# Another order of the first mixer's steps on four engines

## The chip, the cores and the metric

The kernel runs on one core of a Trainium2 chip. A core has a matrix engine (TensorE, PE in the rows, with PEld its weight loads), a vector engine (VectorE, DVE), an engine for functions of one element (ScalarE, ACT), a general one (GpSimd, POOL), and a fifth, SyncE (SP), that here only issues transfers. The metric is the time of one execution on the device in microseconds, the median of three runs.

## The reference, cut to what matters

The program is one block with a three-part mixer and a feed-forward network, and then two layers with three branches each. Only the order of work in the first mixer changes. There 272 tokens of 1024 features are normalised, multiplied by `w_in` and split into three groups:

```python
p = rms_norm(h, norm_mix_pre[l]) @ w_in[l]
pa = p[..., :A_COLS]                  # 512 columns: the LRU group
pb = p[..., A_COLS:A_COLS + B_COLS]   # 1544 columns: forgetting attention, 8 heads
pc = p[..., A_COLS + B_COLS:]         # 1024 columns: RWKV-7, 4 heads
oa = rg_lru_group(xa, ya, ...)        # a convolution, two gates, a scan, gelu
ob = forgetting_attention_group(...)  # softmax(q k + c_i - c_j) v
oc, v_own = rwkv7_group(pc, ...)      # a recurrent state per head
mixed = jnp.concatenate([oa, ob, oc], axis=-1) @ w_out[l]
h = h + rms_norm(mixed, norm_mix_post[l])
```

The recurrence of RWKV-7 is

```python
s_kk = jnp.einsum('bhij,bhj->bhi', S, kk_t)
S = S * w_t[:, :, None, :] - s_kk[..., None] * (kk_t * a_t)[:, :, None, :] + v_t[..., None] * k_t[:, :, None, :]
```

The kernel computes it in chunks of 64 tokens. Five chunks of four heads need the inverse of a triangular 64x64 matrix each, found in five levels of doubling (blocks of 2, 4, and so on up to 64).

## The kernel before, in words

All weights of the matrix products come from memory as units of 128x1024 numbers. SP fetches a unit into `raw`, ACT rounds it to `whi`, DVE (or POOL, for every fourth unit in the mixer) subtracts to get the rest `wlo`, and PE multiplies three times, `xh` by `whi`, `xl` by `whi` and `xh` by `wlo`. These are the steps called `split`, letter w. One output tile of 128 features takes one unit and 24 matmuls. The three products serve to keep float32 accuracy.

The mixer's tiles come in the order C (8 tiles, RWKV), two heads' q and k, v, the other q and k, and A (4 tiles, LRU); then the 8 tiles of `w_out`, called `op`. Between the tiles PE does the small products of the three groups.

No scheduler runs. Each engine executes a list of steps, and the table `WEAVE` holds the order: for each phase and engine one string of letters. `mixer_lines` gives for each letter a line of steps, and `laid` takes the next step of the line that each letter names. So a string fixes how the lines are interleaved on an engine, never the order inside a line. The letters are: d tiles and their evacuations from PSUM, w splits, r the RWKV steps in their order of need, s RWKV steps with time to spare, l and n the LRU, f the forget gates, e and o the attention turns (even and odd, six turns of five parts: scores, maximum and exponentials, reciprocal and normalisation, transposes, values), m token shifts, c the late copies before `w_out`, p the `w_out` tiles, z `beat`.

Semaphores carry the dependences: `wait_ge` in a step waits for named events, `says` announces one. A wait blocks everything that stands behind it on its engine. PSUM has 8 banks. Tiles rotate through three of them, all small products through the other five, and a product waits until its bank's earlier holder was read.

The steps that matter here:

- `enter` ("in", k): for each k of 8, ACT scales `h` to `xh` and squares it, DVE makes `xl`, PE does nine matmuls and sums the squares. `inend` is the square root on ACT and the reciprocal `rr` on DVE, which every evacuation needs.
- `la.a`, `la.c`: constants of the LRU, on ACT (absolute value, exponential, logarithm) and DVE.
- `rw.X`: the first matrix of the inverse, from `rw_be` and `AR`. `rw.inv0`: its transpose `rw_XT`, on POOL. `rw.lb`: the masks of the levels (`rw_x` tiles, from `MA`), the first on DVE, the rest on POOL.
- `rw.leva`, level v: 40 matmuls (20 per half) and two copies on ACT. `rw.levb`: 80 matmuls and four subtractions on DVE from `rw_X` and `rw_XT`, the "level differences".
- `lr.conv`, `lr.exp`, `lr.tan`, `lr.b`, `lr.scan`, `lr.cut`: the LRU group, on DVE, ACT and POOL.
- `rw.pair`, `rw.scanU`, `rw.scanS`, `rw.o`, `rw.mean`, `rw.var`, `rw.fin`, `rw.oc`: the rest of RWKV. `late`: the attention's output copied and split for `w_out`.
- `beat`: 1 to 4 products of a matrix of ones with itself, whose result nobody reads, 12 in the seven that letter z places (BEATS 3, 1, 1, 2, 1, 1, 4), and 4 more inside the first `op` tile. Each is executed as two matmuls in the trace. `pulse` is the same kind of work, 14 products ahead of the feed-forward part.

Of the kernel before, what the change touches and what calls it, by code (L numbers as in the profile page):

```python
# [261 lines left out]
WEAVE = {  # L262
    "mixer": {
        "pe": (
            "ddddddddddfdddddddddrddddddrrdddddddrrrddddfdddddddrrddeddrrrsssdrdrdlrdrdldrddrssrseeessseosoorre"
            "eerrrrrrozrororeroozrerereeozozrorrroeozerrzorzrroppppppppp"
        ),
        "act": (
            "eodwdwdddwwddwdsdndwwwwfwwrwsrwwrwrrrrwrrwwwrrwwdddddwwrrwwserewlrwlwlrdwdresslseesocorrrererooooo"
            "eeceoooeeroerroerrrrroocccpwwpwppwpwpwpwpp"  # L270
        ),
        "dve": (
            "dmwdwdddwwwdddsdnddwddfwwwdmdfdwwmwsrrddmdmmdwwrdwmmwwmddwdrrwrrrrdwwdrsssdfwrrrwerwrrrwddssrdreee"
            "edlrwdlrrwldwwldrrssssslssoolllrroererrrerrororooreroooerrcerereooreoeroorrrrcccpwwpwwpppwpwpwpp"
        ),
        "pool": (
            "wwewwedmoopdddddddwdwwwmmwwwwmmwwwwrrmrmmwwwwrrrwwwwsswrrrwwreeeweerrwwwwllcoooooeeeeeoooooceeeooo"
            "rrcpppwwwwpppp"
        ),
        "sp": (  # L280
            "dwwwwwwwwwwwwwwwwwwwwwwwwwwwwwwwwwwww"
# [7 lines left out]
        "act": (
            "wddddqddwddwbwdwccwccwvwccwvvwccwvvwcwvvccwwvcvwcwvcwvcwcwvvwcwvvcwcwvcvwcwvcwvcwcwvvwcwvvcwccvwvw"  # L290
            "cwvcvwcwcvwvcwcwvvwqccwvvwcvwqvqccwcvwvwcvwcvcwwvcvwvwvwvbwwwwwwwwwww00w00w01w00111111000001111w1w"
            "wrrr"
        ),
        "dve": (
            "hwdhhhhdhddhhddwddwwdddwddwcdwcdwvcwdcdwvcwdcwdvcdwcwdvcwdcwdvwcdwcdwvcdwcwdvcwdcwdvcwdcwdvwcdwcdw"
            "vcwdcwdvcwdcdvwcwdcwvdcwdcwdvwcdwcdwvcwdcdwvcdwcvwdcdwcdvwcwdcvwdcdwcwdvcwcvwccvwwwwwwwwwwwww0000w"
            "0011w0101110w1101000011111www"
        ),
# [13 lines left out]
        "act": (
            "aeoswwwwwwtwtwwtwwweedwdddodowdwedddowwdwdeeowdowdeedwweoodweedeeowdwboodeoeeodwweedwdwwwwwwwoooew"
            "essssosssowwowwoddddwsdwdwsdwdwdwdwdwdwdwdwdwdwdwdwdwdwdwdwdwdwwwmwmwwmwmwwmwmwwmwmbwwww000w00w1w0"
            "11011110001111100wrrwwr"
        ),
        "dve": (
            "ddwwdwdwdwdwdwttddwwdwdwdeeowdeeowdodddddwwowdwydwyeodwydeoyewdeeyodwwyoeedeywedoyewodwooydeoyeedw"
            "weedyyuwwuwuwuwwwowoosseowssssosswowwoddddsdwwdsdwwdwdwdwdwdwdwdwdwdwdwdwdwdwdwdwdwdwddwddwddwmddw"
            "mddwddwmddwmddwddwmddwmddwddwmwmwwww0000w0011w11011001110000w111110www"  # L320
        ),
# [13 lines left out]
        "act": (
            "aoewswwwwtwwtwwtwwweeddddoodwdewdddowwwdwdeeooweewddeooweewdeoedwdwoodbeoeeowdeeowwwoodeoeodwowdww"
            "wowwwswssssswswwdsddddwwsdwdwdwdwdwdwdwdwdwdwdwdwdwdwdwdwdwdwdwwwmmwwwmwmwwmwmwwmmbwwww0000011111"
        ),
# [2405 lines left out]
```

How the kernel before makes its waits and increments, by code:

```python
    def wait_ge(self, *events):  # L118
        if self.book.counting:
            return
        for ev in events:
            name, val = self.book.value[ev]
            if self.met.get(name, 0) < val:
                self.e.wait_ge(self.book.sem(name), val)
                self.met[name] = val
# [612 lines left out]
            def bank(banks, key):  # L738
                b, before = book.take(banks, key)
                if before is not None and not book.counting:
                    pe.wait_ge(*book.freed_by[before])
                return tiles[b]
# [1 line left out]
            def take(n=1):  # L744
                u, i = divmod(at[0], 8)
                at[0] += n
                if u == 0 and i == 4 or u and i == 0:
                    pe.wait_ge(("w.hi", u), ("w.lo", u))
                c = slice(128 * i, 128 * (i + n))
                return whi[:, u % NSPL, c], wlo[:, u % NSPL, c], [("w.used", u)] if at[0] % 8 == 0 else []
# [1 line left out]
            def dense(o, xs, event, first=True, last=True):  # L752
                for i, (a, b, evs) in enumerate(xs):
                    hi, lo, said = take()
                    pe.wait_ge(*evs)
                    mm(o, hi, a, first and i == 0, False)
                    mm(o, hi, b, False, False)
                    t = mm(o, lo, a, False, last and i == len(xs) - 1)
                    if last and i == len(xs) - 1:
                        said = [event] + said
                    if said:
                        t.then_inc(*pe.says(*said))
```

## Time and profile before

| what | value |
|---|---|
| median of three runs | 941.23 us (940.35 to 943.87) |
| the profiled execution, from its first to its last instruction | 940.6 us |
| PE busy | 918.4 us, 98% of the span |
| DVE busy | 696.6 us, 74% |
| ACT busy | 521.6 us, 55% |
| POOL busy | 226.8 us, 24% |
| the mixer, to the end of the last `w_out` tile | 0 to 196 us |

The page gives the profiled execution no time other than this span. A row of a timeline gives start, duration, engine, line and operation, and in brackets the idle time before it with what ended it. Since the ends of matmuls are modelled, idle time of PE is better read from brackets and from starts than from the busy sum. Most DVE and POOL rows carry the line of a helper (L1713, L1717, L1718, L1721, L2306), so the tiles' names tell the steps apart.

### The profile page before, as it was taken

Reading aid. Unit: us, or ns where it says so; the run is one execution under the profiler, and the core shown is the slowest. Engines: PE = TensorE matmul, PEld = TensorE weight load, DVE = VectorE, ACT = ScalarE, POOL = GpSimd, SP = SyncE. Lnnn points to the kernel's source line nnn. Section 1 sums busy time; section 2 is a strip of 40 time slices with the busy share of each in tenths; the row PEclk is TensorE's granted clock in tenths of the full one; section 3 lists DMA queues with packets and bytes.
Section 4 is the critical chain, followed back from the end, with each engine's and each line's share of the span. In section 5 each row is a group of like instructions: output and inputs, shape, how many; then the busy total and the mean of one; then the engine's idle time right before and its main releaser. Section 6 shows DMA issues by size and latency. Waiting matters only on the chain.

```text
span 940.6 us, 19615 instructions
## 1 busy us (share of the span) xinstructions
PE 918.4 (98%) x7924; PEld 855.0 (91%) x7924; DVE 696.6 (74%) x1072; ACT 521.6 (55%) x942; POOL 226.8 (24%) x194
## 2 busy tenths in 40 slices
PE   8999999989999999999999999999899999999997
PEld 7999887979999988789999899998699998999995
DVE  6988875477999896578788695586768787665684
ACT  8653464446655664464665475545646665555442
POOL 2445321441212221004222040032023122410240
PEclk9999999999999999999999999999999999999999
DMA  8543200235555555456544446555284435555451
GB/s 320 180 157 113 70 26 2 68 113 180 183 189 185 184 178 180 170 176 245 179 140 153 152 136 203 192 188 181 100 305 152 146 125 177 183 178 181 159 201 45
DMA packets 41705, 150.32 MB, mean 160 GB/s; under 512 B 4624, under 2 KB 5008, under 8 KB 41360
## 3 DMA queue, kind: packets, MB, share of 16 engines
q1 hardware_dynamic: 39600, 141.54, 44.7%
q10 hardware_dynamic: 2016, 7.54, 2.1%
q8 instruction: 63, 1.03, 0.4%
q14 instruction: 26, 0.21, 0.1%
HBM read 148.01 MB, written 1.05 MB: 158 GB/s over the span
## 4 chain that ended last, share of the span: by engine, by line
PE 89%; DVE 4%; ACT 2%; issue 2%; DMA 1%; POOL 1%; DVEq 0%; SPq 0%; ACTq 0%; POOLq 0%
PE ps L736 87%; PE ps L1073 2%; DVE wlo L1713 1%; DMA raw<-in_ws 1%; DVE S L1713 1%; ACT whi L1297 1%; PE ps L1189 0%; DMA h<-in_hT 0%; ACT xh L1297 0%; DVE xl L1721 0%; POOL ocf L2306 0%; ACT L1297 0%; ACT tmp L1297 0%; DVE ht L1721 0%; DVE pcraw L1713 0%
## 5 line engine op out<-in xcount | busy, mean ns | idle before, releaser
L1297 ACT ACTIVATE whi<-raw 128x1024 fp32r<-128x1024 f32 (+1 forms) x265 | 278.2, 1052 | 282.1 <-PE ps L736 276.5
L736 PE MATMUL ps<-xh,whi 128*128 128x256 f32 (+2 forms) x1440 | 412.9, 287 | 4.5 <-ACT xh L1297 1.8
L736 PE MATMUL ps<-xl,whi 128*128 128x256 f32 (+2 forms) x1440 | 407.9, 283 | 2.3 <-DVE xl L1721 2.2
L736 PE MATMUL ps<-xh,wlo 128*128 128x256 f32 (+2 forms) x1440 | 407.0, 283 | 0.0
L1713 DVE TENSOR_TENSOR wlo<-raw,whi 128x1024 fp32r<-128x1024 f32 (+1 forms) x257 | 328.0, 1281 | 103.8 <-ACT whi L1297 103.1
L736 PEld LDWEIGHTS ps<-xh,whi 128*128 128x128 f32 x1440 | 271.5, 189 | 10.9 <-issue 8.3
L736 PEld LDWEIGHTS ps<-xl,whi 128*128 128x128 f32 x1440 | 270.9, 188 | 3.9 <-DVE xl L1721 3.5
L736 PEld LDWEIGHTS ps<-xh,wlo 128*128 128x128 f32 x1440 | 272.0, 189 | 0.0
L736 PE MATMUL ps<-yh,whi 128*128 128x256 f32 x232 | 65.3, 282 | 0.0
L736 PE MATMUL ps<-yl,whi 128*128 128x256 f32 x232 | 65.2, 281 | 0.0
L736 PE MATMUL ps<-yh,wlo 128*128 128x256 f32 x232 | 65.2, 281 | 0.0
L2306 POOL TENSOR_TENSOR gts<-gts 128x256 f32<-128x256 f32 x32 | 33.2, 1047 | 132.0 <-DVE gts L1721 131.4
L2306 POOL TENSOR_TENSOR al<-cv,ah 128x256 fp32r<-128x256 f32 x22 | 30.2, 1374 | 117.3 <-ACT ah L1297 117.3
L736 PE MATMUL ps<-whi,xh 128*128 128x512 f32 x128 | 51.4, 401 | 2.2 <-ACT xh L1297 1.4
L736 PE MATMUL ps<-whi,xl 128*128 128x512 f32 x128 | 50.6, 395 | 1.5 <-DVE xl L1721 1.5
L736 PE MATMUL ps<-wlo,xh 128*128 128x512 f32 x128 | 50.4, 394 | 0.0
L2306 POOL TENSOR_TENSOR yl<-tmp,yh 128x256 fp32r<-128x256 f32 x24 | 25.6, 1076 | 101.6 <-ACT yh L1297 101.6
L1721 DVE SCALAR_TENSOR_TENSOR cv<-ev,col,cv 128x256 f32<-128x256 f32 x88 | 48.5, 552 | 1.6
L736 PEld LDWEIGHTS ps<-yh,whi 128*128 128x128 f32 x232 | 43.7, 188 | 0.0
L736 PEld LDWEIGHTS ps<-yl,whi 128*128 128x128 f32 x232 | 43.7, 188 | 0.0
L736 PEld LDWEIGHTS ps<-yh,wlo 128*128 128x128 f32 x232 | 43.7, 188 | 0.0
L1713 DVE TENSOR_TENSOR gts<-ps,rr 128x256 f32<-128x256 f32 x54 | 22.4, 421 | 24.6 <-PE ps L736 23.4
(345 smaller groups left out, 1317.7 us busy)
## 6 DMA issues: line engine op xcount, KB each, us to landing
raw<-in_ws SPq DMA_DIRECT2D x261, 512.0 KB, 3.4
h<-in_rel ACTq DMA_DIRECT2D x2, 1024.0 KB, 13.2
qc<-in_gam ACTq DMA_DIRECT2D x3, 512.0 KB, 4.6
mt<-in_m ACTq DMA_DIRECT2D x2, 768.0 KB, 7.7
h<-in_hT SPq DMA_DIRECT2D x4, 272.0 KB, 5.2
raw<-in_ws SPq DMA_DIRECT2D x4, 256.0 KB, 2.8
gts<-in_lng ACTq DMA_DIRECT2D x2, 512.0 KB, 10.0
out<-ht SPq DMA_DIRECT2D x4, 256.0 KB, 2.4
```

Of the source, the lines that this page charges most:

```text
L736: return e.matmul(o, l, r, start=start, stop=stop, skip_group_check=True)
L1073: w = e.transpose(ps[0:kn, x * 128:x * 128 + nq], S[t % 2][0:nq, x, k0:k0 + kn], ident[0:nq, 0:nq])
L1297: return e.activation(o, a, f, bias=bias, scale=scale, accum_out=acc)
L1713: return e.tensor_tensor(o, a, b, op)
L1721: return e.scalar_tensor_tensor(out=o, in0=a, scalar=s, in1=b, op0=op0, op1=op1)
L2306: return e.tensor_tensor(o, a, b, op)
```

## The change

Only the four strings of the mixer for PE, DVE, ACT and POOL are new. The strings of the other three phases are the same; where they stand in the diff, the entries of DVE and ACT have merely changed places in the dictionary. SP's string is the same. Every instruction of before is there once, on the same engine; the number of function table loads on ACT is 25 in both.

```diff
@@ WEAVE["mixer"]
         "pe": (
-            "ddddddddddfdddddddddrddddddrrdddddddrrrddddfdddddddrrddeddrrrsssdrdrdlrdrdldrddrssrseeessseosoorre"
-            "eerrrrrrozrororeroozrerereeozozrorrroeozerrzorzrroppppppppp"
+            "ddddddddddfddddddrddddddddrrddddrrrfddddddddrrddddddddrrreddddsssdeddddrlrrlerreddrsssrsssoersrero"
+            "orrrrrorroreoooreerereerooroorrreererroorrozzzzzpppppppppzz"
         ),
...
```

On PE, `rw.X` comes right behind the last v tile and `rw.M` one and a half tiles earlier than before. Six half tiles of A (three tiles) stand ahead of `leva` of level 1, where one half tile stood. Before, a half tile of A stood between the steps of a level; now the first two levels have only `lr.gate` between theirs, and the last tile of A stands inside the third.

The entry, on ACT. Before, the end of the entry stood as follows (`xh` and `tmp` are the last k, `lam` is `la.a`, `rr` the square root):

```order
L1297 ACTIVATE whi<-raw 128x1024
L1297 ACTIVATE xh<-h,col 128x272
L1297 ACTIVATE tmp<-h 128x272
L1297 ACTIVATE wfh<-mt 128x64
L1297 ACTIVATE xh<-h,col 128x272
L1297 ACTIVATE tmp<-h 128x272
L1297 ACTIVATE lam<-col 128x2
L1297 ACT_TABLE_LOAD
L1297 ACTIVATE lam<-lam 128x2
L1297 ACT_TABLE_LOAD
L1297 ACTIVATE lam<-lam,ones 128x2
L1297 ACT_TABLE_LOAD
```

Now it is:

```order
L1297 ACTIVATE xh<-h,col 128x272
L1297 ACTIVATE tmp<-h 128x272
L1297 ACTIVATE xh<-h,col 128x272
L1297 ACTIVATE tmp<-h 128x272
L1297 ACTIVATE whi<-raw 128x1024
L1297 ACTIVATE wfh<-mt 128x64
L1297 ACTIVATE rr<-ps,epsc 128x272
L1297 ACTIVATE whi<-raw 128x1024 x4
```

The three `lam` steps with their table loads stand behind the split of unit 16 now, and the last two k are ahead of the fourth split.

The inverse's first level, on DVE. Before (`xa` the evacuation of a tile of A, `pcraw<-xa` the convolution `lr.conv`, `rw_X` and `rw_XT` the level differences, `rif` a reciprocal of the attention's first turn):

```order
L1713 TENSOR_TENSOR rw_x<-MA,k 128x640
L1713 TENSOR_TENSOR kT<-ps,rr 128x272
L2006 TENSOR_REDUCE nmf<-fS 16x4
L2010 RECIPROCAL rif<-smf 16x4
L1713 TENSOR_TENSOR xa<-ps,rr 128x272
L1718 TENSOR_SCALAR pcraw<-xa,col 128x272
L1721 SCALAR_TENSOR_TENSOR pcraw<-xa,col,pcraw 128x272 x3
L1713 TENSOR_TENSOR rw_X<-rw_X,ps 128x320
```

Now:

```order
L1713 TENSOR_TENSOR xa<-ps,rr 128x272
L2006 TENSOR_REDUCE nmf<-fS 16x4
L1718 TENSOR_SCALAR pcraw<-xa,col 128x272
L1721 SCALAR_TENSOR_TENSOR pcraw<-xa,col,pcraw 128x272 x3
L1713 TENSOR_TENSOR xa<-ps,rr 128x272
L2010 RECIPROCAL rif<-smf 16x4
L1713 TENSOR_TENSOR rw_x<-MA,k 128x640
L1718 TENSOR_SCALAR pcraw<-xa,col 128x272
L1721 SCALAR_TENSOR_TENSOR pcraw<-xa,col,pcraw 128x272 x3
L1713 TENSOR_TENSOR rw_X<-rw_X,ps 128x320
```

Both convolutions and both evacuations stand ahead of the first level difference, and the first turn's reciprocal stands behind the second tile of A. On POOL, at the same place (`fS<-fS,rif` is the normalisation that waits for that reciprocal, `rw_XT` is `rw.inv0`, `rw_x` the masks):

```order
 L2306 TENSOR_TENSOR rw_bee<-rw_a,rw_pe 128x640
-L2306 TENSOR_TENSOR rw_pe<-rw_k,rw_pe 128x640
-L2306 TENSOR_TENSOR wlo<-raw,whi 128x1024
+L2306 TENSOR_TENSOR fS<-fS,rif 16x4x16
 L2306 TENSOR_TENSOR rw_XT<-MA,k 128x640
 L2306 TENSOR_TENSOR rw_XT<-k,rw_XT 128x640
-L2306 TENSOR_TENSOR rw_x<-MA,k 128x640 x2
-L2306 TENSOR_TENSOR fS<-fS,rif 16x4x16
-L2306 TENSOR_TENSOR rw_x<-MA,k 128x640 x2
```

The normalisation has moved ahead of `rw.inv0` and of the masks.

The end of the mixer's small products, on PE. Before (`ones` is `beat`, `cst,fS` transposes of attention, `fPT,vk` its values, `xh,whi` the first `w_out` tile):

```order
L736 MATMUL ps<-k,rw_pe 128x2 x3
L736 MATMUL ps<-ones 128x128 x4
L736 MATMUL ps<-cst,rw_Y 128x128 x2
L736 MATMUL ps<-cst,rw_Y 128x16
L736 MATMUL ps<-cst,rw_XT 128x128 x2
L736 MATMUL ps<-cst,rw_XT 128x16
L736 MATMUL ps<-fPT,vk 64x128 x12
L736 MATMUL ps<-xh,whi 128x258
```

Now:

```order
L736 MATMUL ps<-cst,rw_Y 128x128 x2
L736 MATMUL ps<-cst,rw_Y 128x16
L736 MATMUL ps<-cst,rw_XT 128x128 x2
L736 MATMUL ps<-cst,rw_XT 128x16
L736 MATMUL ps<-fPT,vk 64x128 x12
L736 MATMUL ps<-ones 128x128 x8
L736 MATMUL ps<-xh,whi 128x258
```

Of the seven beats, which stood one by one among the scan steps and the last attention turns, five (8 products) stand together ahead of the first `w_out` tile and two (5 products) behind the last, next to `pulse`.

Three more moves are spoken of below. On DVE, `fo.lr` (the four writes to `LRb`) and `rw_be` stand ahead of the evacuations of three v tiles; before, `fo.lr` came after `rw_be`. The splits 25 and 26, which stood around `lr.exp` ahead of `lr.tan`, are behind the scores of the sixth attention turn, and POOL's split 27, which came during `lr.tan`, is behind the fourth turn's normalisation. In the last turns ACT does `lr.cut`, `rw.o` 0 and `late` 0 ahead of the sixth turn's exponentials, and both `rw.mean` and both `rw.var` ahead of the copy of the fifth turn's output.

## Rows read from the trace of the kernel before

**Rows 1.** The page: its head, and busy time of each engine.
```profile
span 940.6 us, 19615 instructions
...
PE 918.4 (98%) x7924; PEld 855.0 (91%) x7924; DVE 696.6 (74%) x1072; ACT 521.6 (55%) x942; POOL 226.8 (24%) x194
```
**Rows 2.** Stretches: length, busy by engine (x instructions), granted clock, DMA share, GB/s.
```profile
20.00:100.00 80.00, 79.55 (x782) 74.67 (x779) 68.25 (x101) 42.72 (x66) 34.61 (x22) 1.00 0.42 138
...
160.00:180.00 20.00, 18.73 (x173) 17.02 (x170) 8.13 (x16) 10.65 (x26) 6.17 (x6) 1.00 0.01 2
...
220.00:240.00 20.00, 20.00 (x170) 20.00 (x169) 17.77 (x29) 13.67 (x21) 2.48 (x2) 1.00 0.56 185
```
**Rows 3.** Timeline of PE, entry: start, duration, what, idle before and releaser.
```profile
11.00 0.36 PE L736 MATMUL ps<-xh,whi 128*128 128x272 f32 x1 [0.87 <-DVE wlo L1713]
...
16.71 0.39 PE L736 MATMUL ps<-xl,whi 128*128 128x272 f32 x1 [0.51 <-DVE xl L1721]
...
23.02 0.40 PE L736 MATMUL ps<-xh,whi 128*128 128x272 f32 x1 [0.45 <-DVE pcraw L1713]
```
**Rows 4.** Timeline of ACT and DVE at the end of the entry.
```profile
18.75 1.28 ACT L1297 ACT_TABLE_LOAD   x1
20.04 0.49 ACT L1297 ACTIVATE rr<-ps,epsc 128x272 f32<-128x272 f32 x1
...
20.56 1.85 DVE L1755 RECIPROCAL rr<-rr 128x272 f32<-128x272 f32 x1 [1.56 <-ACT rr L1297]
```
**Rows 5.** Timeline of PE, the two waits inside the inverse.
```profile
117.53 0.54 PE L736 MATMUL ps<-AR,rw_pi 64*64 64x128 f32 x5 [1.35 <-DVE rw_X L1713]
...
129.94 0.35 PE L736 MATMUL ps<-rw_X,rw_x 64*64 64x64 f32 x5 [0.53 <-DVE rw_X L1713]
```
**Rows 6.** Timeline of DVE (`lr.tan`) and POOL in 109 to 117 us.
```profile
110.56 1.67 DVE L1717 TENSOR_SCALAR xa<-pcraw 128x272 f32<-128x272 f32 x1
...
114.15 2.57 DVE L1721 SCALAR_TENSOR_TENSOR pcraw<-pcraw,xa 128x272 f32<-128x272 f32 x1
...
109.70 2.38 POOL L2306 TENSOR_TENSOR rw_x<-MA,k 128x640 f32<-128x640 f32 x1 [8.05 <-PE ps L736]
114.08 2.35 POOL L2306 TENSOR_TENSOR wlo<-raw,whi 128x1024 fp32r<-128x1024 f32 x1 [2.00 <-ACT whi L1297]
```
**Rows 7.** Timeline of DVE: the four writes of `fo.lr`.
```profile
73.78 1.96 DVE L1718 TENSOR_SCALAR LRb<-ps,k 128x272 f32<-128x272 f32 x4
```
**Rows 8.** Timeline of POOL (`rw.inv0`) and of PE (`leva` of level 1).
```profile
88.02 1.57 POOL L2306 TENSOR_TENSOR rw_XT<-MA,k 128x640 f32<-128x640 f32 x1
89.67 2.02 POOL L2306 TENSOR_TENSOR rw_XT<-k,rw_XT 128x640 f32<-128x640 f32 x1
...
90.50 1.38 PE L736 MATMUL ps<-rw_X,rw_x 64*64 64x64 f32 x40
```
**Rows 9.** Timeline of DVE, ACT, POOL and PE in the last turns.
```profile
151.99 0.74 DVE L2006 TENSOR_REDUCE nmf<-fS 128x4 f32<-128x576 f32 x1
...
158.73 0.40 ACT L1297 ACTIVATE rw_bee<-ps 128x272 f32<-128x272 f32 x1 [4.27 <-PE ps L736]
...
172.89 0.96 POOL L2306 TENSOR_TENSOR xl<-qT,xh 128x272 fp32r<-128x272 f32 x1
...
174.00 0.36 PE L736 MATMUL ps<-xh,whi 128*128 128x258 f32 x1 [1.26 <-POOL xl L2306]
```
**Rows 10.** PE's groups in 139 to 170 us (busy, mean ns), and its timeline.
```profile
L736 PE MATMUL ps<-ones 128*128 128x128 f32 x26 | 4.5, 293 | 0.0
...
171.69 1.05 PE L736 MATMUL ps<-ones 128*128 128x128 f32 x8
...
201.79 0.36 PE L736 MATMUL ps<-xh,whi 128*128 128x258 f32 x1 [1.12 <-ACT xh L1297]
```
**Rows 11.** Stretches around the fall of the clock (columns as in rows 2).
```profile
151.20:154.60 3.40, 3.40 (x36) 2.27 (x37) 1.89 (x8) 1.94 (x10) 0.00 (x0) 1.00 0.00 0
154.60:158.00 3.40, 3.40 (x47) 2.70 (x49) 2.85 (x6) 0.00 (x0) 1.15 (x1) 0.50 0.02 5
```

More of the change, by code:

```diff
@@ L264 @@
         "pe": (
-            "ddddddddddfdddddddddrddddddrrdddddddrrrddddfdddddddrrddeddrrrsssdrdrdlrdrdldrddrssrseeessseosoorre"
-            "eerrrrrrozrororeroozrerereeozozrorrroeozerrzorzrroppppppppp"
+            "ddddddddddfddddddrddddddddrrddddrrrfddddddddrrddddddddrrreddddsssdeddddrlrrlerreddrsssrsssoersrero"
+            "orrrrrorroreoooreerereerooroorrreererroorrozzzzzpppppppppzz"
+        ),
+        "dve": (
+            "dwdwdmdwdddwdsdddddwwmmwdwmfmddmwwwdrdrwdmdrfwwwrrrrrdrddwwwmfrdddwwrrwmrrdssrrrewddwwssnssddelder"
+            "rlrwewdrrllrsessslssoorrdorererrrrrreoorrrooerlooollrreeereoowwosreerrroorrccccpppwwwwwpppwwpwpp"
         ),
         "act": (
[L269 to L274, printed above, removed]
+            "dwedwddwddwdddwsdwwwwrrrwwworfwwwrrrrrrwwwnswwrrrddddwwwwwwsdeerlrllrdersswwweesoosrldrrerooooeeee"
+            "ooooeecrrcoreorrrrerroocccppwwppwwwwpppwpp"
         ),
         "pool": (
-            "wwewwedmoopdddddddwdwwwmmwwwwmmwwwwrrmrmmwwwwrrrwwwwsswrrrwwreeeweerrwwwwllcoooooeeeeeoooooceeeooo"
-            "rrcpppwwwwpppp"
+            "dwwdddmdddddwwowwwwmmwwmrewwrwwmmmwmrwwwwrrrwwwwwwwseerrrrrsrwoooeeeeeooopooowwwolwwleeeeeeooooccr"
+            "recpppwppwpwwp"
         ),
@@ L288 @@
         ),
+        "dve": (
+            "hwdhhhhdhddhhddwddwwdddwddwcdwcdwvcwdcdwvcwdcwdvcdwcwdvcwdcwdvwcdwcdwvcdwcwdvcwdcwdvcwdcwdvwcdwcdw"
+            "vcwdcwdvcwdcdvwcwdcwvdcwdcwdvwcdwcdwvcwdcdwvcdwcvwdcdwcdvwcwdcvwdcdwcwdvcwcvwccvwwwwwwwwwwwww0000w"
+            "0011w0101110w1101000011111www"
+        ),
         "act": (
@@ L292 @@
             "wrrr"
[L293 to L297, printed above, removed]
         ),
@@ L311 @@
         ),
+        "dve": (
+            "ddwwdwdwdwdwdwttddwwdwdwdeeowdeeowdodddddwwowdwydwyeodwydeoyewdeeyodwwyoeedeywedoyewodwooydeoyeedw"
+            "weedyyuwwuwuwuwwwowoosseowssssosswowwoddddsdwwdsdwwdwdwdwdwdwdwdwdwdwdwdwdwdwdwdwdwdwddwddwddwmddw"
+            "mddwddwmddwmddwddwmddwmddwddwmwmwwww0000w0011w11011001110000w111110www"
+        ),
         "act": (
@@ L315 @@
             "11011110001111100wrrwwr"
[L316 to L320, printed above, removed]
         ),
@@ L334 @@
         ),
[L335 to L338, printed above, removed]
         "dve": (
@@ L342 @@
             "wdwddwdmdwddmwddwdwddwdmdmwdmwmwwww00000001111111"
+        ),
+        "act": (
+            "aoewswwwwtwwtwwtwwweeddddoodwdewdddowwwdwdeeooweewddeooweewdeoedwdwoodbeoeeowdeeowwwoodeoeodwowdww"
+            "wowwwswssssswswwdsddddwwsdwdwdwdwdwdwdwdwdwdwdwdwdwdwdwdwdwdwdwwwmmwwwmwmwwmwmwwmmbwwww0000011111"
         ),
```

## The prediction

> **What bounds the kernel now.** I read the page first: PE is busy 918.4 of 940.6 us [rows 1], so only PE's idle time can be won, 22 us in the whole program. Then the stretches of the mixer [rows 2]: between 20 and 100 us PE has 79.55 of 80 us, and nothing is to be won there, only lost. At the end of the small products PE has 18.73 of 20, and time lies there. Third, PE's timeline, for what ended its idle time. In the entry there are three waits of 0.87, 0.51 and 0.45 us [rows 3]. In the inverse there are two, 1.35 and 0.53 us, both for a level difference `rw_X` of DVE [rows 5]. Ahead of the first `w_out` tile there is one of 1.26 us, for the last `xl` of POOL [rows 9]. Last, the beats: in 139 to 170 us 26 matmuls of ones make 4.5 us of PE busy time [rows 10]. They do no work for the result, so PE has slack there, and in that stretch the end is set by a chain through DVE, ACT and POOL.
>
> All the rest of the program runs the same lists as before, so the change is worth what it moves the moment at which the first `w_out` tile has its inputs (174.00 us, rows 9), plus what it changes behind the last one.
>
> **The entry.** The three waits make 0.87 + 0.51 + 0.45 = 1.83 us [rows 3]. The first goes for the most part, because ACT now rounds unit 1 ahead of the next k. The second goes, because the seventh k is no longer behind the fourth split. The third came from `rr`: the square root at 20.04 us stood exactly behind a table load of 1.28 us that began at 18.75 [rows 4], and with `la.a` gone it starts when PE's sums are there; then the reciprocal of 1.85 us follows as before. What is late next is `xl` of the last k, because on DVE it stands behind `init2`, and that waits for ACT's copy behind the fourth split: I take 0.6 us for what comes back. So the entry is worth -1.2 us; the bounds are -1.83 and 0.
> The Trainium skill ("ScalarE: Activation LUTs", section "What ACT_TABLE_LOAD costs") says that a switch costs the load of 1.28 us and about as much again in a drain. The trace has the load but no drain: 18.75 + 1.28 is 20.03, and the square root starts at 20.04. By the page the entry would gain about 1.3 us more; by the row it doesn't, and I go by the row.
>
> **Ahead of `rw.X`.** PE now wants `rw.X` as soon as the last v tile ends, some 9 us sooner than before. It needs `rw_be`, and on DVE that stands behind the four writes of `fo.lr`, 1.96 us [rows 7], and behind two steps of k on POOL. PE has no work ahead of this point that it could bring forward, so a late `rw_be` is idle PE. If DVE comes in time the cost is 0; if all of `fo.lr` is in the way it is 1.96. I take the middle, rounded down for the work that PE still has in the last v tile: +0.9.
>
> **The first levels of the inverse.** POOL's normalisation of the first turn waits for a reciprocal that DVE does only after the second tile of A, and `rw.inv0` is queued behind it. It is two operations of 1.57 and 2.02 us [rows 8], the second with 0.4 to 0.5 us of waiting in it. From the second tile of A to `levb` of level 1 PE has a tile of A (24 matmuls; dense tiles pass at 170 in 20 us, rows 2, so 2.8 us), `leva` (1.38, rows 8) and the four matmuls of `lr.gate`, so a good 4.2 us. Against it stand on POOL the small normalisation and 1.57 + 2.02, and between them `lb` of level 1 and the convolution on DVE. In the trace such DVE operations on SBUF tiles don't run beside one of POOL: the two of `lr.tan` took 1.67 and 2.57 us, to 112.23 and 116.72, and the POOL operations beside them ended at 112.08 and 116.43 [rows 6]. So the two engines take turns, and `rw.inv0` ends about 1 us after PE wants it (estimated: 3.6 us of its own and three DVE operations between, against 4.2 and the gate). Then the rest of the convolution takes turns with two masks, which puts the first level difference, and so `leva` of level 2, some 0.7 us late. I take 1.2 + 0.7 = +1.9. The bounds are 0 (PE's work covers all of it) and 3.6 (`rw.inv0` all bare).
> The Trainium skill ("SBUF — State Buffer", section "SBUF: two separate sides") makes this an exclusive lock that whichever starts first holds for its whole instruction, and this speaks against the change; were it only a slowing of both, the term would be about 0.3. Rows 6 are of the first kind.
>
> **The two waits that go.** `lr.tan` no longer meets POOL's split 27, and splits 25 and 26 are out of its way. Its two stretched operations, 1.67 + 2.57 = 4.24 us [rows 6], shrink by most of that, so the third level's differences are there before PE has done `rw.M`. Both waits go: -1.35 - 0.53 [rows 5] = -1.9, with 0 as the other bound, if the last mask on POOL still meets `lr.tan`.
>
> **The last turns.** Here PE isn't the bound, so what is won or lost ahead of it counts only as far as the chain starts sooner. By the terms so far PE is 0.3 us early (-1.2 + 0.9 + 1.9 - 1.9). The chain runs from the maxima of one attention turn (151.99 us for the fifth, rows 9) over exponentials, normalisation, transposes and values to the next, and beside it RWKV's output. ACT in it sat idle 4.27 us until 158.73, waiting for `rw.o` [rows 9]. PE ran `rw.o` in a stretch in which its clock was granted at 0.50 [rows 11], that is 1.2 GHz: at 2.4 GHz it is done up to 1.7 us sooner. The order behind it is tighter too: both roots of `rw.var` ahead of the output copy. What ends last is POOL's `xl` (172.89 + 0.96 = 173.85), which starts PE at 174.00 [rows 9]. I take -1.1 for this stretch, together with the 0.3 from above -1.4, with bounds of 0 and -2.5.
>
> **The beats.** The eight products ahead of the first `w_out` tile run as 16 matmuls; eight take 1.05 us [rows 10], so about 1.9 us. They stand where PE waited 1.26 us anyway, and that wait moves rather than grows since the attention's values end sooner as well: 0, at worst +1.9 - 1.26 = +0.6. The five behind the last tile, 1.2 us, stand where PE was idle 1.12 us [rows 10]: 0.
>
> **The clock.** Among the small products it fell once, at 154.6 us [rows 11], after a stretch that shows PE busy for its whole length and held the small products of the turns. The beats that stood among them are gone, so at least that much will happen again: such a stretch costs between 0 and half its length, 1.7 us. I take one with +0.4 and the upper bound for three with +5.
>
> **Sum.** -1.2 + 0.9 + 1.9 - 1.9 - 1.1 + 0 + 0.4 = -1.0 us against the profiled execution's 940.6, 939.6. The median of the runs stood 0.6 above it (941.23), so the time to expect is 940.2.
>
> **Rivals.**
> *The last turns absorb everything.* The chain restarts at the attention turns, and they stand in nearly the same order on ACT and DVE: the mixer ends at 174 us whatever came before. For it: the 4.5 us of beats [rows 10] show that PE's progress isn't what counts there. Against it: the last link of the chain, ACT behind `rw.o`, was slowed by the clock and not by the order. Time: 941.2.
> *Slower: the small products without beats lose the clock.* One mechanism, in 140 to 169 us. The stretch of rows 11 was lost even with beats. Without them three or four such stretches may follow each other, each up to 1.7 us, in which matmuls of the chain itself take double. It decides from the second such stretch on. Price: three at 1.1 us on average (a part of each falls on waits), 3.3 us: 943.5.
> *The gain is larger.* The waits that I fear in the inverse don't come (0.9 + 1.9 us less), and the clock holds (0.4): 940.2 - 3.2 = 937.0. For it: between 20 and 100 us DVE is busy 68.25 of 80 us and PE hardly ever waited for it [rows 2], so DVE has some room. Against it: `rw.inv0` behind a reciprocal is a plain order, not a matter of load.
>
> **Chances.** Forecast 0.45, absorbed 0.2, slower 0.2, larger gain 0.15. A measurement of this kernel can tell 0.5% from no change, 4.7 us; all four cases lie inside it, and only their tails leave it: 0.09 faster, 0.07 slower, 0.84 within. The forecast's own range is 938.5 to 942.0, from the halves of the bounds above. The range that holds 8 in 10 reaches from 936.5 to 944.0; it takes in the larger gain and the slower case's middle.
>
> **What would show it.** Right, if in the profile of the changed kernel PE has no idle bracket above 0.5 us before the ninth matmul group of the entry except one for the last `xl`, and the square root starts about 1.1 us sooner than 20.04; if PE waits 0.5 to 2 us for POOL's `rw_XT` ahead of level 1 and about 1 us ahead of `rw.X`; if the waits of rows 5 are gone; and if the first `w_out` tile gets its inputs at 172 to 173 us. Wrong, if PE runs through the inverse without a wait, if the granted clock is 0.50 for more than two stretches in 140 to 170 us, or if anything differs behind 200 us.

## The result: 946.7 us against 941.2, slower, and outside the predicted range

The changed kernel takes 946.69 us (median of 4 executions, 945.74 to 949.51); the kernel before, on the same chip, 941.24 (4 executions, 940.35 to 943.87). The ratio is 1.0059, 95% interval 1.0043 to 1.0075. Predicted were 940.2 us and a range of 936.5 to 944.0, and the chance for slower by over 0.5%, which this is, was put at 0.07. The profiled execution took 946.85 us with a span of 945.1.

The page after, its head and the busy times: as many matmuls, 4.5 us more span, of which 4.2 us are busy time of PE.
```profile
span 945.1 us, 19613 instructions
...
PE 922.6 (98%) x7924; PEld 858.7 (91%) x7924; DVE 695.8 (74%) x1072; ACT 520.7 (55%) x942; POOL 229.4 (24%) x194
```
The same matmuls take longer, and the mean granted clock is 0.989 where it was 0.996. The loss is found by setting the start of the same step of PE in both traces side by side (after minus before, us):

| step of PE | before | after | difference |
|---|---|---|---|
| first C tile, behind the entry | 23.02 | 23.21 | +0.19 |
| `rw.pair` G, end of the inverse | 138.52 | 136.34 | -2.18 |
| `at f 4 0` | 148.98 | 147.79 | -1.19 |
| `rw.scanS 3` | 150.36 | 150.93 | +0.57 |
| `rw.mean 0` | 160.26 | 163.40 | +3.14 |
| second `w_out` tile | 176.23 | 177.86 | +1.63 |
| feed-forward, entry step 0 | 201.79 | 203.56 | +1.77 |
| feed-forward, entry step 4 | 211.60 | 214.54 | +2.94 |
| first layer, third value tile | 405.59 | 410.09 | +4.50 |

So the inverse ended sooner, and that was lost again at four places: one wait of 1.7 us, a slow piece behind it, and two more in the feed-forward's and the first layer's entry, where both kernels have the same order.

**The entry.** PE's brackets in 10 to 24 us (columns as in rows 3) answer to [rows 3]:
```profile
10.78 0.36 PE L736 MATMUL ps<-xh,whi 128*128 128x272 f32 x1 [0.38 <-DVE wlo L1713]
18.48 0.39 PE L736 MATMUL ps<-xl,whi 128*128 128x272 f32 x1 [1.17 <-DVE xl L1721]
```
The three waits became two, of 1.55 us together instead of 1.83, and the root `rr` starts at 20.24 instead of 20.04 [rows 4]. The last `xl` is late because DVE's `init2` stands ahead of it, and that operation took 2.35 us beside a split on POOL (0.79 us before):
```profile
15.57 2.37 POOL L2306 TENSOR_TENSOR wlo<-raw,whi 128x1024 fp32r<-128x1024 f32 x1
...
15.67 2.35 DVE L1713 TENSOR_TENSOR wfl<-mt,wfh 128x64 fp32r<-128x64 f32 x1 [0.81 <-ACT wfh L1297]
17.94 0.49 DVE L1721 SCALAR_TENSOR_TENSOR xl<-h,col,xh 128x272 fp32r<-128x272 f32 x1
```
Before, the same split had stretched the seventh k's `xl` to 2.31 us (from 14.34 us), and the second wait of [rows 3] came from that. So this stretch was moved, not removed.

**The inverse.** Ahead of `rw.X` and ahead of the first level PE has no bracket at all. One is left, ahead of level 2 (PE, then DVE and POOL beside it):
```profile
103.74 1.50 PE L736 MATMUL ps<-rw_X,rw_x 64*64 64x64 f32 x40 [0.86 <-DVE rw_X L1713]
...
98.08 5.11 DVE L1721 SCALAR_TENSOR_TENSOR pcraw<-xa,col,pcraw 128x272 f32<-128x272 f32 x3
...
97.96 1.54 POOL L2306 TENSOR_TENSOR rw_XT<-k,rw_XT 128x640 f32<-128x640 f32 x1
99.47 3.43 POOL L2306 TENSOR_TENSOR rw_x<-MA,k 128x640 f32<-128x640 f32 x2
```
Three DVE operations of the convolution took 5.11 us in turns with POOL (1.58 before, from 94.91 us). Both waits of [rows 5] are gone: `rw.M 1 1` and `leva` of level 5 have no bracket. The two operations of `lr.tan` that took 1.67 and 2.57 us [rows 6] take 0.29 and 0.44 without POOL beside them; a mask on POOL (from 110.09 us) meets the operation ahead of them instead:
```profile
110.17 1.81 DVE L1721 SCALAR_TENSOR_TENSOR pcraw<-pcraw 128x272 f32<-128x272 f32 x1
...
111.91 0.29 DVE L1717 TENSOR_SCALAR xa<-pcraw 128x272 f32<-128x272 f32 x1
...
114.12 0.44 DVE L1721 SCALAR_TENSOR_TENSOR pcraw<-pcraw,xa 128x272 f32<-128x272 f32 x1
```
The waits and the entry make 0.19 + 0.86 - 1.35 - 0.53 = -0.83 of the 2.18 us by which `rw.pair` G comes sooner. The other 1.35 us are busy time of PE, from the first C tile to `rw.pair` G, with the same work (columns as in rows 2; before, then after). Why PE needs less for it in the new order stays open:
```profile
23.02:138.52 115.50, 113.62 (x1589) 106.75 (x1590) 96.85 (x151) 60.73 (x111) 45.30 (x30) 1.00 0.34 111
...
23.21:136.34 113.13, 112.27 (x1588) 106.41 (x1590) 88.81 (x149) 62.30 (x109) 40.25 (x25) 1.00 0.30 99
```

**The wait.** DVE, POOL and PE in 146 to 151 us. On DVE the LRU's two scans now stand between `rw.scanS 2` and `rw.scanU 3`, and on POOL split 27 stands just ahead of its part of them:
```profile
146.29 4.40 DVE L2095 TENSOR_TENSOR_SCAN pcraw<-pcraw 128x272 f32<-128x272 f32 x2
150.62 0.26 DVE L1713 TENSOR_TENSOR rw_k<-ps,rw_a 128x128 f32<-128x128 f32 x1
...
147.06 2.33 POOL L2306 TENSOR_TENSOR wlo<-raw,whi 128x1024 fp32r<-128x1024 f32 x1
149.36 0.74 POOL L2306 TENSOR_TENSOR pcraw<-pcraw,lora 128x272 f32<-128x272 f32 x1
...
150.93 0.45 PE L736 MATMUL ps<-rw_k,rw_lw 64*64 64x64 f32 x8 [1.69 <-DVE rw_k L1713]
```
Each scan by itself, before and after (shortest, mean and longest in ns, then the starts):
```profile
L2095 DVE TENSOR_TENSOR_SCAN pcraw<-pcraw x2: 699/712/724, 128.1 to 128.7; 128x272 f32<-128x272 f32 x2
...
L2095 DVE TENSOR_TENSOR_SCAN pcraw<-pcraw x2: 725/2244/3764, 146.3 to 146.9; 128x272 f32<-128x272 f32 x2
```
The second took 3.76 us: it lies beside both POOL operations, which end at 150.10 us, and ends 0.59 us behind them, at 150.69. The scan step's `rw_k` is queued behind it, and PE waits 1.69 us.

**The clock.** Stretches (columns as in rows 2), cut where the granted clock changes:
```profile
148.75:152.17 3.42, 1.43 (x28) 1.03 (x26) 3.38 (x6) 0.21 (x1) 2.11 (x3) 1.00 0.00 0
152.17:155.58 3.41, 3.13 (x22) 1.98 (x21) 1.81 (x5) 2.10 (x10) 0.00 (x0) 0.50 0.00 0
155.58:159.00 3.42, 3.42 (x32) 2.01 (x29) 1.97 (x6) 0.44 (x2) 1.15 (x1) 0.50 0.00 0
159.00:162.41 3.41, 3.41 (x70) 3.41 (x68) 3.18 (x3) 1.16 (x4) 0.00 (x0) 0.50 0.08 16
...
203.37:206.78 3.41, 1.77 (x11) 1.21 (x9) 3.38 (x5) 0.35 (x2) 2.56 (x3) 1.00 0.29 107
206.78:210.19 3.41, 2.48 (x12) 2.52 (x13) 3.34 (x7) 3.12 (x8) 1.65 (x2) 0.50 0.12 47
210.19:213.61 3.42, 3.42 (x16) 3.23 (x16) 2.72 (x7) 1.83 (x4) 0.75 (x1) 0.50 0.00 0
...
401.35:404.76 3.41, 1.95 (x9) 1.25 (x10) 3.41 (x9) 2.85 (x8) 0.00 (x0) 1.00 0.45 154
404.76:408.17 3.41, 3.41 (x10) 2.54 (x9) 2.79 (x5) 0.00 (x0) 0.00 (x0) 0.50 0.21 77
```
PE was busy for 1.43 of the 3.42 us from 148.75 to 152.17 us, and then ran at 1.2 GHz for 10.2 us, against 3.4 us before [rows 11]. `rw.o` is in it: ACT's copy of it comes at 161.25 us instead of 158.73 [rows 9]. At the two later entries the half-clock time is 6.8 and 3.4 us; before it was 3.4 and none. Towards the last inputs of `w_out` the new order wins some back: the last `xl` of POOL ends at 175.48 us (173.85 in rows 9), 1.6 us late, where `rw.mean 0` was 3.1 us late.

### The profile page after: what moved, and what is told of

Its sections match the earlier page's. It is cut to its first block, busy times and chain, and to the rows that moved or that the text cites. A ratio compares the mean times of both kernels' runs of the same rounds, so it can differ in the third digit from the quotient of the medians.

```text
span 945.1 us, 19613 instructions
## 1 busy us (share of the span) xinstructions
PE 922.6 (98%) x7924; PEld 858.7 (91%) x7924; DVE 695.8 (74%) x1072; ACT 520.7 (55%) x942; POOL 229.4 (24%) x194
## 4 chain that ended last, share of the span: by engine, by line
PE 90%; DVE 5%; ACT 2%; issue 1%; DMA 1%; SPq 0%; DVEq 0%; ACTq 0%
PE ps L736 88%; PE ps L1073 2%; DVE wlo L1713 1%; DVE S L1713 1%; DMA raw<-in_ws 1%; ACT whi L1297 1%; DVE pcraw L2095 0%; DVE xl L1721 0%; PE ps L1189 0%; DVE pcraw L1721 0%; ACT L1297 0%; DVE rw_x L1721 0%; ACT xh L1297 0%; DVE wfl L1713 0%; DVE ht L1721 0%
```

## The experiments

All were timed in five rounds beside the kernel before, whose medians there were 941.2 to 942.0 us. An edit of an order is a few letters moved in an engine's string; it is shown here by the names of the steps that do something on that engine. Names beginning with a_ start from the changed kernel, with b_ from the one before. The microseconds given as a gain are differences of medians, often of different rounds; the ratios compare executions of the same rounds. Where the executions of a kernel spread, the two differ by up to 2 us, and then both are given.

**First: the wait, or the beats?**

a_beats_back:
```diff
 pe (changed kernel)
+ beats 0..6 ahead of: rw.scanS 0, rw.scanS 2, at f 3 4, rw.scanU 4, at f 4 4, at f 5 3, rw.fin 0
- beats 0..4 ahead of op 0, beats 5, 6 behind opend
```


> The changed kernel with its seven beats back among the last turns (before rw.scanS 0, rw.scanS 2, at f 3 4, rw.scanU 4, at f 4 4, at f 5 3 and rw.fin 0), nothing else changed. Theory of the beats (they kept TensorE's clock full between 140 and 169 us): the three stretches at half clock from 152.2 us become one or none, the first w_out tile comes 1.2 to 1.6 us earlier, and the time is about 944 to 945 us. Theory of the stall (the 1.7 us in which TensorE waits for the second scan step, 149.24 to 150.93 us, is what loses the clock): the stretches stay, and the time is 946.5 us within 0.8 us. Either way it shows whether the stretches at the feed-forward's and the first layer's entry (206.8 and 404.8 us) stand as they are.


948.78 us (ratio 1.0074, 1.0052 to 1.0096): 2.1 us worse than the changed kernel. The wait ahead of `rw.scanS 3` is still there, now 2.35 us, and so are three stretches at half clock behind it; a fourth has come at 143.2 us. So in this order the cause is not that the beats are missing from their old places, none of which lies in that wait.

b_beats_end:
```diff
 pe (kernel before)
- the seven beats among the turns
+ beats 0..4 ahead of op 0, beats 5, 6 behind opend
```


> The kernel before with only the beats moved to their new places (five ahead of the first w_out tile, two behind opend), nothing else changed. Theory of the beats: the clock falls for two or three stretches between 145 and 170 us instead of one, and the time is 942.5 to 945 us. Theory of the stall: the clock's stretches in the mixer stay as they are, the turns lose the beats' own time where the row is not waiting, and the time is 941.2 us within 0.7 us.


947.32 us (1.0063, 1.0039 to 1.0088): 6 us worse than the kernel before, outside both expectations. In its profile half-clock time rose from 3.4 to 10.2 us in the mixer and from 3.4 to 6.8 in the feed-forward's entry. So in the old order the beats did hold the clock. My rival on the beats was right for the old order and wrong for the new one.

a_split27_early and a_scans_early:
```diff
 pool, both runs
   at f 1 2
+  split 27
   at f 2 2
   at f 3 2
-  split 27
   lr.scan 0
 a_scans_early also: lr.b, lr.scan 0, lr.scan 1 behind at f 1 1 (dve), ahead of at f 1 2 (pool), lr.b behind rw.pair bt (act)
```


> The changed kernel with only GpSimd's split 27 moved, from between at f 3 2 and lr.scan 0 to behind at f 1 2 (about 129.5 us). If split 27 is what stretches VectorE's lr.scan 1 from 0.70 to 3.76 us, it falls to about 1.5 us (lr.scan 0 on GpSimd still lies beside it), and the step rw.scanS 3 begins 1.5 us earlier: same gain as with the recurrence moved as well. If the recurrence itself in the chain is the price, the gain is under half of that kernel's.

> The changed kernel with the LRU's recurrence (lr.b, lr.scan 0 and 1 on VectorE, their evictions on ScalarE and GpSimd) back behind the first turn, as before, and GpSimd's split 27 ahead of that of at f 2 2. Theory of the stall: lr.scan 1 takes 0.7 us again instead of 3.76, rw.scanS 3 on TensorE begins 1.5 to 1.8 us earlier (about 149.3 us), at least two of the three stretches at half clock from 152.2 us go, the first w_out tile comes 2 to 3 us earlier, and the time is 943 to 944.5 us, or 940 to 941 us if the stretches at the two later entries go as well. Theory of the beats: the wait goes, the half-clock stretches stay, the gain is 1 us or less (945.5 to 946.5 us).


942.58 us (0.9999, 0.9981 to 1.0016) with split 27 alone, 944.22 (1.0025, 1.0011 to 1.0040) with the recurrence moved as well. One POOL step moved (split 27; the letters of 26 and 28, which do nothing on POOL, moved with it) takes 4.1 us off, 0.60% or 5.6 us by the ratios, which is the whole loss. The scans (DVE), the scan step's `rw_k`, and the PE step that waited, in the profile of a_split27_early:
```profile
147.60 1.39 DVE L2095 TENSOR_TENSOR_SCAN pcraw<-pcraw 128x272 f32<-128x272 f32 x2
148.92 0.26 DVE L1713 TENSOR_TENSOR rw_k<-ps,rw_a 128x128 f32<-128x128 f32 x1
...
149.82 0.45 PE L736 MATMUL ps<-rw_k,rw_lw 64*64 64x64 f32 x8
```
1.39 us for both instead of 4.40, and no bracket on PE. Moving the recurrence forward as well gives part of the gain back: `rw.pair` G comes at 137.65 us instead of 136.33. So what the late position of the recurrence cost, it cost through split 27 beside it; that it is a gain otherwise is suggested by the 1.6 us between the two medians, though their intervals overlap. The executions of a_split27_early part by their clock: three at 938.0 to 938.5 us with a mean granted clock of 0.998, nine at 941.4 to 944.7 us with 0.988 to 0.991. Those of the kernel before with 0.998 take 940.5 to 941.8. So at the same clock the order is worth 2 to 3 us, and the clock takes it away in most executions. The profiled one (942.36 us) shows where: there is no wait of PE ahead of `rw.scanS 3` any more, and still the mixer has 10.2 us at half clock, as much as the changed kernel's. Two of its three stretches, each with the one ahead of it:
```profile
139.36:142.77 3.41, 2.55 (x56) 1.79 (x50) 3.02 (x7) 0.38 (x1) 2.00 (x1) 1.00 0.00 0
142.77:146.18 3.41, 3.41 (x22) 2.73 (x24) 1.58 (x7) 1.79 (x10) 0.00 (x0) 0.50 0.00 0
...
149.60:153.01 3.41, 3.11 (x46) 2.13 (x42) 2.72 (x7) 1.19 (x6) 0.67 (x1) 1.00 0.00 0
153.01:156.42 3.41, 3.41 (x39) 2.27 (x37) 2.43 (x6) 1.56 (x8) 1.15 (x1) 0.50 0.00 0
```
So that one wait is not all that lowers the clock in the scan steps.

b_scans_late, the reverse edit:
```diff
 (kernel before)
 dve:  rw.scanS 2
+      lr.b, lr.scan 0, lr.scan 1
       rw.scanU 3
 pool: at f 3 2
+      split 27, lr.scan 0, lr.scan 1, lr.cut
 act:  + lr.cut ahead of late 0
```


> The kernel before with only the LRU's recurrence put late as in the changed kernel: lr.b, lr.scan 0 and 1 on VectorE behind rw.scanS 2, GpSimd's split 27, lr.scan 0 and 1 and lr.cut behind at f 3 2, ScalarE's lr.cut ahead of late 0. Theory of the stall: lr.scan 1 takes over 2.5 us beside split 27, TensorE waits 1 to 2 us ahead of rw.scanS 3, a stretch at half clock or two are added behind it, and the time is 943 to 945.5 us. Rival (the stall only costs where beats are gone as well): it is within 1 us of 941.3 us.


946.20 us (1.0040, 1.0027 to 1.0052). The loss came, 0.7 us above the range that I gave, and not where I said: the scans took 1.34 us together, split 27 stretched a step of `rw.scanS 2` (2.65 us), and DVE's `late 0` waited 1.90 us for its copy ahead of the turn's first operation. PE, and the stretches around:
```profile
152.06 0.61 PE L736 MATMUL ps<-fPT,vk 16*64 16x16 f32 x8 [1.24 <-ACT fPT L1297]
...
148.25:151.67 3.42, 2.21 (x30) 1.55 (x27) 1.52 (x4) 1.27 (x4) 2.68 (x4) 1.00 0.41 143
151.67:155.08 3.41, 2.72 (x22) 2.30 (x24) 3.16 (x8) 0.95 (x6) 1.48 (x2) 0.50 0.01 2
```
In this kernel, too, the half clock lasts three stretches. And it has the gain of the inverse in full: `rw.pair` G at 136.33 us, with the A tiles, levels and entry of the kernel before.

**Second: is it the idle time that loses the clock?** This run changes neither the wait nor any order of real work:
```diff
 pe (changed kernel)
+ beat 0, now 7 products instead of 3, ahead of rw.scanS 3
- beat 0 ahead of op 0
```


> The changed kernel, split 27 and all orders untouched, but the first beat (now seven products, 1.6 us) stands ahead of rw.scanS 3, where TensorE waits 1.7 us for VectorE; the other beats as in the changed kernel. The wait itself stays, so nothing gets earlier by the order. If TensorE's idleness in it is what loses the clock, at most one stretch at half clock is left between 150 and 165 us and the time is 943 to 945 us; if the thin steps behind it lose the clock, or the lateness itself is the price, the three stretches stay and it is 946.2 to 947.5 us.


943.35 us (1.0007, 0.9990 to 1.0024), 3.3 us less than the changed kernel. PE, and the first of the stretches that follow:
```profile
149.48 1.83 PE L736 MATMUL ps<-ones 128*128 128x128 f32 x14
151.24 0.45 PE L736 MATMUL ps<-rw_k,rw_lw 64*64 64x64 f32 x8
...
150.45:153.86 3.41, 2.83 (x40) 2.04 (x38) 3.34 (x8) 0.41 (x2) 0.76 (x1) 1.00 0.00 0
153.86:157.27 3.41, 3.41 (x65) 2.58 (x65) 1.83 (x7) 2.35 (x10) 1.15 (x1) 1.00 0.02 5
```
`rw.scanS 3` starts as late as in the changed kernel, and the clock stays at 2.4 GHz to 164.1 us; one stretch at half clock is left in the mixer. By the ratios the gain is 0.52%, 4.9 us. Filling the wait thus gives most of what taking it away gave (4.1 us by the medians, 5.6 by the ratios): here PE's idleness in the wait cost more than the lateness of the step behind it.

**Third: the later entries.** Three runs fill PE's waits in the feed-forward's first entry step and in each layer's first value tiles:
```diff
+                    if st and k == 0 and j == 0:
+                        fill(ps_of(("pulse", st)), 8)
                     pe.wait_ge(("x.lo", st, k))
...
+                if st and k == 0:
+                    fill(ps_of(("pulse", st)), 4)
+
+            def fill(ps, n):
+                for _ in range(n):
+                    mm(ps[:, 0:128], ones, ones, True, True)
...
+                if b == 0 and i == 2:
+                    fill(ps_of(("vc", l, 1)), 3)
...
+                    if b == 0 and k == 0:
+                        fill(ps_of(("vc", l, 1)), 3)
                     pe.wait_ge(("x.lo", 2 + l, k, b))
```


> The changed kernel with split 27 early, beats untouched, and idle time of TensorE at three later entries filled with 128x128 products: eight in the 1.9 us wait for x.lo in the feed-forward's first entry step and four behind it, and three and three in the waits of each layer's first value tiles (0.9 us each). If the half-clock stretches at those entries (two in the changed kernel's feed-forward entry, one at 404.8 us, one at 668 us in this order) come from that idle time, they go, and the time falls from 942.6 to 939.5 to 941 us. If they only follow the stretches lost in the mixer, nothing changes but the products' own time (0 to 0.5 us more).

> The kernel before with only the idle time at the three later entries filled (twelve products in the feed-forward's first step, six in each layer's). It has one half-clock stretch at the feed-forward's entry in the profile (205.8 us). If idle time loses it: 1 to 1.4 us less, 940 to 940.5 us, and the executions at 943 to 945 us become rarer. If the products cost as much as the clock gives back, 941.3 us within 0.5 us.

> The changed kernel with only the idle time at the three later entries filled. In its profile 1.2 us of the 4.5 us are lost in the feed-forward's entry and 1.6 us in the first layer's, at half clock. If both go by the products: 943.5 to 944.5 us, and what remains over the kernel before (2 to 3 us) is the mixer's stall and its three stretches. If only the phase of the mixer's stretches sets the later ones, 946.7 us within 0.7 us.


On a_split27_early the filling gives 940.41 us (0.9987, 0.9972 to 1.0001), 2.2 less; on the kernel before 940.64 (0.9984, 0.9973 to 0.9996), 1.0 less; on the changed kernel 945.00 (1.0022, 1.0010 to 1.0035), 1.7 less. By the ratios it is 1.1, 1.5 and 3.5 us; for a_split27_early the two intervals overlap. The last two lie between what I expected in one case and in the other. In none of the three profiles is a stretch at these entries at half clock. So what was lost there is a matter of PE's idle time at the entries, not of the mixer. The mixer's stretches are still there in a_fill (10.2 us from 152.0 us, one more at 169); in b_fill, whose mixer is that of the kernel before, there is none, so a single profile's count of them is that of one execution. Why the changed kernel loses more there than the kernel before, with the same instructions in both, stays open. The moment within the entry at which the clock is lowered differs from trace to trace (3.2 us after entry step 0 begins in the changed kernel, 4.0 in the kernel before); that this decides it was not tested.

**Fourth: beats only where PE waits.**
```diff
 a_s27_beats: a_split27_early + the beats as in a_beats_back
 a_s27_gaps:  a_split27_early + BEATS (2, 2, 1, 2, 1, 1, 4, 4), beats 0..2 ahead of rw.scanU 1, rw.scanU 2, at f 3 4
 a_s27_gaps_fill: a_s27_gaps + the filled entries
 a_s27_gaps2_fill: BEATS (2, 2, 3, 1, 1, 1, 4, 4), beats 0..3 ahead of rw.scanU 1, rw.scanU 2, at f 2 4, at f 3 4
```


> The changed kernel with GpSimd's split 27 early (942.58 us as it stood alone) and the seven beats back among the last turns as in the kernel before. If what is left of the loss (nine of twelve executions at 941.4 to 944.7 us with a mean granted clock of 0.988 to 0.991, three at 938.0 to 938.5 us with 0.998) is that the last turns without beats lose the clock, most executions go to about 0.996 and the time to 938.5 to 940.5 us. If beats only lengthen the chain of scan steps (alone, on the changed kernel, they cost 2.1 us), it is 943 to 945 us.

> As a_s27_beats, but beats only where TensorE waits anyway among the scan steps: two products ahead of rw.scanU 1, two ahead of rw.scanU 2, one ahead of at f 3 4 (waits of 0.49, 0.37 and 0.30 us in the trace), the other four beats as in the changed kernel. If the clock in 138 to 152 us is lost for these waits, the time is 939 to 941 us; if it is lost for the thin turns from 152 us on, it stays at 942.6 us within 0.7 us.

> The changed kernel with all three remedies: split 27 early, beats only in TensorE's waits among the scan steps, entries filled. Sum of the parts measured: 946.7 - 4.1 (split 27) - 0.9 (beats in the waits) - 2.2 (entries) = 939.5 us, so 938.5 to 940.5 us, which would be faster than both kernels. If the stretches at half clock at 152 us stand, as in the profiles of a_s27_gaps and a_s27_fill, it is not below 940.4 us.

> a_s27_gaps_fill with three more products in TensorE's 0.82 us wait ahead of at f 2 4 (taken from the beats ahead of the first w_out tile). If that wait loses the clock in 5 of its 12 executions (939.6 to 943.0 us), most of these go to 938 us and the median to 937.8 to 938.6 us; if not, 939.0 us within 0.5 us.


In the old places 943.28 us (1.0011, 0.9995 to 1.0027): no gain. Its executions at a clock of 0.996 to 0.997 take 940.1 to 942.6 us, against 938.0 to 938.5 of a_split27_early at 0.998, so I take it that the beats lengthen the chain where PE has no wait. In the waits 941.68 (0.9992, 0.9974 to 1.0009), a difference of 0.9 that the spread doesn't bear out, and between my two expectations. With the entries filled 938.96 (0.9970, 0.9954 to 0.9985): faster than both kernels. Three more products ahead of `at f 2 4` change nothing that can be told: 939.61 (0.9973, 0.9960 to 0.9987), with a smaller spread (937.96 to 941.28 against 937.67 to 943.00).

**Fifth: which part of the new order carried the gain?** Starting from the kernel before, only the LRU's recurrence, split 27 and the copies that wait for the recurrence go late:
```diff
 b_scans_late_s27: b_scans_late, but split 27 behind at f 1 2
 b_lru_late:       and lr.cut behind at f 4 1 (act), lr.cut, late 0 behind at f 5 2 (pool), late 0 ahead of late 1 (dve, act)
 b_lru_late2:      but act's late 0 behind rw.o 1
 b_lru_late_fill, b_lru_late2_fill: with the filled entries
```


> The kernel before with the LRU's recurrence late (as in b_scans_late, 946.2 us) but GpSimd's split 27 early, behind at f 1 2; the beats in their old places. If the gain of the changed kernel's inverse (2.2 us by rw.pair G) comes from the recurrence and split 27 no longer standing ahead of the differences of rw.levb 4 and of rw.M 1 1, and not from the A tiles, the levels' order or the entry, then this kernel has it too (rw.pair G at 136.3 to 136.8 us instead of 138.5), without the wait ahead of rw.scanS 3, and takes 939 to 941 us. If the rest of the new order carries the gain, or the thin turns lose the clock here as well, it is 941.5 to 943.5 us.

> The kernel before (its entry, A tiles, levels and beats untouched) with the LRU's recurrence late, split 27 behind at f 1 2, and the copies that wait for the recurrence late as well (ScalarE's lr.cut behind at f 4 1, GpSimd's lr.cut and late 0 behind at f 5 2, late 0 on VectorE and ScalarE with late 1). If these moves alone carry the gain of the new order, rw.pair G comes at 136.3 to 136.8 us, no wait over 0.7 us is left between 148 and 153 us, and the time is 938.5 to 940.5 us. If the A tiles, the levels and the entry carried part of it, it is 940.5 to 942 us.

> b_lru_late with the filled entries of b_fill (which took 1.0 us off the kernel before): 937.5 to 939.5 us if the two add; equal to a_s27_gaps_fill (938.96 us) within 0.7 us if both orders do the same work with the same waits.


944.34 us (1.0021, 1.0011 to 1.0032), 943.41 (1.0019, 1.0002 to 1.0035) and 943.32 (1.0011, 0.9998 to 1.0023): three misses, in each of which the profile shows a wait that was only moved. In the first, DVE's `late 0` stood ahead of `at f 4 0` and waited for the copies, 149.78 us instead of right behind `rw.scanU 3` at 147.87. In the other two PE reached `at f 5 4` at 165.3 to 165.7 us (before: 169.26) and then stood, as PE's timeline of b_lru_late shows:
```profile
173.50 0.55 PE L736 MATMUL ps<-xh,whi 128*128 128x258 f32 x1 [4.34 <-POOL xl L2306]
```
ACT's `late 0` stood behind `at f 5 4`, and POOL's `rw.fin` queued behind the `late 0` that waited for it. With that one step forward:

> b_lru_late (943.4 us) with ScalarE's late 0 behind rw.o 1 instead of behind at f 5 4, so that GpSimd's late 0 runs in its idle time ahead of rw.fin 0. If the recurrence and its copies carry the gain, the 4.3 us wait in the first w_out tile falls to 1 us or less, and the time to 939 to 940.5 us, faster than the kernel before. If GpSimd's rw.fin steps keep the tile waiting, 941 to 942.5 us.

> The same with the filled entries: 938 to 939.5 us if this moved recurrence is all that was worth having in the new order, since a_s27_gaps_fill, with the new order whole, takes 938.96 us. Over 940 us would say that the A tiles, the levels' order or the beats' new places carry part of it.


939.79 us (0.9976, 0.9963 to 0.9989) and 938.31 (0.9962, 0.9947 to 0.9977), the fastest of all and the most even (938.12 to 938.70). The wait in the first `w_out` tile, forecast at 1 us or less, is 1.38 us in b_lru_late2 and 1.37 in b_lru_late2_fill:
```profile
170.59 0.36 PE L736 MATMUL ps<-xh,whi 128*128 128x258 f32 x1 [1.37 <-POOL xl L2318]
```
So moving the recurrence and its copies is enough to reach, with filled entries, what the whole new order reaches with the same remedies (938.31 against 938.96). The A tiles ahead of the inverse, the order of the levels and the entry brought nothing that can be told apart here. Of the 2.9 us over the kernel before, the fillings alone gave 1.0 there (b_fill).

## Why the prediction was wrong

- **"The clock", the step that failed.** The sum took one half-clock stretch and +0.4 us, with +5 as the upper bound. The trace has three in the mixer; filling the wait alone took off 3.3 us, filling the later entries 1.7 (4.9 and 3.5 by the ratios, which is more than the loss of 5.5, so they need not add; both together were not run). The upper bound of +5 had the size, but the range ended at 944.0. The slower rival had the place (140 to 169 us), the number of stretches and nearly their price right (3.3 us; by the table above 2.6), and its cause wrong: not the missing beats (putting them back cost 2.1 us), but in the main PE's idleness in the wait behind the scan. What else lowers the clock in the scan steps, where it fell in a_split27_early without that wait, stays open.
- **"All the rest runs the same lists, so the change is worth what it moves at the first `w_out` tile".** False: of the 4.5 us, 2.7 arise behind it, at 206 to 214 and at 404 to 408 us. Such entries have idle PE time, and whether the clock falls there isn't fixed by their code, which is the same in both.
- **"The last turns", -1.4 with the lead.** The mechanism wanted was a chain that starts sooner. I wrote that these steps stand in nearly the same order on DVE; in fact lr.b, both scans and POOL's split 27 had moved into the chain. The difference went from -1.19 to +0.57 us there. I had described that stretching of DVE beside POOL for another place [rows 6], and didn't look for it here. Taking split 27 out of the chain brings the time back to that of the kernel before (ratio 0.9999).
- **The entry, -1.2.** Measured +0.19, outside its bounds. That `init2` would hold the last `xl` was seen, but it was priced at 0.6 us; PE waited 1.17 us for that `xl`, since POOL's split now stretched `init2`. The cause of the second wait was misread: it was that same split, not the place of the fourth split on ACT.
- **Ahead of `rw.X`, +0.9**: 0, PE never waited. **First levels, +1.9**: a single wait of 0.86 us, for the second part of the mechanism (the convolution in turns with POOL); `rw.inv0` was in time.
- **The two waits, -1.9**: right in size and sign. The cause was half seen. The wait of 1.35 us goes with split 27 leaving `lr.tan`; the one of 0.53 stood behind the scans, which on DVE came ahead of level 4's differences. Put back there in the new order (a_scans_early), the recurrence brings a wait of 0.40 us at that place and `rw.pair` G 1.3 us later. That the inverse ended 2.18 us sooner is in part luck: 1.35 us of it are in no term.
- **The beats, 0**: right in the new order, where those ahead of `w_out` lie before POOL's last `xl` (175.48). Taking them away from their old places cost 6 us in the old order; in the new one putting them back cost 2.1.
- **DVE and POOL in turns.** What rows 6 showed was borne out: the scan of 0.70 us took 3.76 beside two POOL operations, and one split moved away gave 4.1 us. The Trainium skill ("SBUF — State Buffer", section "SBUF: two separate sides") says that the loser of the shared port waits for the other's whole instruction; the trace agrees (POOL's second operation ended at 150.10 us, the scan 0.59 us behind it).
- **The table load.** The root of the entry starts at 20.24 us without a load ahead of it, 20.04 with one; it waits for PE's sums now, so taking the load away gained nothing there. The Trainium skill ("ScalarE: Activation LUTs", section "What ACT_TABLE_LOAD costs") has a drain of about 1.4 us besides the load. The trace disagrees: before, the last `lam` step ended at 18.72 us, the load ran from 18.75 to 20.03, and the root started at 20.04 [rows 4].
